# Moving 64 token steps of a router tile to the next stage, in a hybrid decoder kernel with single-neuron experts

## The reference, cut to what matters

```
def peer(x, w_q, keys, u_tab, v_tab):
    ...
        q = einsum('td,de->te', xb, w_q)                     # 8 heads, two halves
        s = einsum('thcd,hcnd->thcn', q, keys)               # 128 scores per half
        sv, si = lax.top_k(s, 16)                            # top 16 of each half
        cv, ci = lax.top_k(all sums of two halves, 16)       # 16 experts per head
        idx = i1 * 128 + i2
        gate = softmax(cv)
        act = gelu(einsum('thkd,td->thk', u_tab[idx], xb))   # dot with a row of u per expert
        return einsum('thkd,thk->td', v_tab[idx], gate * act) # weighted sum of rows of v
```

## Time and profile before

| | us |
|---|---|
| median of 3 runs (5188.72 to 5211.97) | 5198.52 |
| the profiled execution | 5198.58 |
| its span | 5196.8 |
| mean granted TensorE clock | 0.802 |
| busy PE / DVE / POOL | 3423.1 / 3351.0 / 2704.2 |

### The profile page before, as it was taken

One profiled execution on the slowest core, in us unless ns is written; L12 is line 12 of the kernel. 1 busy time (PEld: TensorE's weight loads), 2 busy tenths in 40 slices (PEclk: granted clock), 3 DMA queues, 4 the chain that ended last, 5 costly groups with the idle time before them and its releaser, 6 DMA issues. The chain is left out here.

```text
span 5196.8 us, 52661 instructions
## 1 busy us (share of the span) xinstructions
PE 3423.1 (66%) x17388; PEld 1932.9 (37%) x17388; DVE 3351.0 (64%) x7219; ACT 726.6 (14%) x2591; POOL 2704.2 (52%) x2288
## 2 busy tenths in 40 slices
PE   7887466699785666566499977467566536656206
PEld 6574352354551541442244463163154113211001
DVE  4345896578535985786577543797687657785480
ACT  2131210111310210200122121110111010000000
POOL 1000566466433775774365534466676565426676
PEclk9998678799887778778699988787777765578658
DMA  5543678899766889999799757789998986759768
GB/s 192 170 143 114 216 239 323 295 401 351 286 243 251 318 311 372 352 322 354 273 352 333 287 212 291 292 278 346 377 337 322 356 307 221 279 205 386 262 222 332
DMA packets 467260, 1497.00 MB, mean 288 GB/s; under 512 B 60096, under 2 KB 122240, under 8 KB 454416
## 3 DMA queue, kind: packets, MB, share of 16 engines
q0 software_dynamic: 324864, 1141.04, 59.6%
q1 hardware_dynamic: 120912, 330.01, 17.2%
q10 hardware_dynamic: 21216, 22.60, 1.3%
HBM read 1480.07 MB, written 55.29 MB: 295 GB/s over the span
## 5 line engine op out<-in xcount | busy, mean ns | idle before, releaser
L2027 POOL DMA_INDIRECT e_ring<-peer_u,e_idx x1152 | 1458.7, 1266 | 1090.9 <-issue 526.6
L2027 POOL DMA_INDIRECT e_ring<-peer_v,e_idxT x1104 | 1196.5, 1084 | 1025.2 <-PE e_ff L2179 509.8
L2063 DVE CUSTOM_DVE_ANT_0 e_ring<-e_ring,e_x 128x1024 f32<-128x1024 f32 (+1 forms) x1152 | 1380.4, 1231 | 302.6 <-DMA e_ring<-peer_u,e_idx 294.8
L2179 PE MATMUL e_ff<-e_ring,e_strips 128*32 128x512 f32 x4416 | 726.3, 756 | 611.8 <-DMA e_ring<-peer_v,e_idxT 500.9
L351 PE MATMUL p_ps<-p_hT,p_w 128*128 128x256 f32 (+2 forms) x1728 | 567.6, 483 | 0.0
L2179 PEld LDWEIGHTS e_ff<-e_ring,e_strips 128*32 128x32 f32 x4416 | 163.8, 126 | 1066.9 <-issue 1065.1
L351 PEld LDWEIGHTS p_ps<-p_hT,p_w 128*128 128x128 f32 x1728 | 327.6, 195 | 208.1 <-issue 129.5
L1314 PE MATMUL bank<-wbuf,kqb 128*128 128x512 f32 (+1 forms) x544 | 278.1, 666 | 101.3 <-DMA wbuf<-w_out 101.1
L1400 PE MATMUL bank<-wbuf,kqb 128*128 128x512 f32 (+1 forms) x576 | 275.5, 628 | 21.5 <-DMA wbuf<-wc 21.5
L375 PE MATMUL p_ps<-p_w,p_hT 128*128 128x512 f32 (+1 forms) x576 | 253.5, 603 | 0.0
L1816 DVE MAX8 top<-kb_kdec 128x8 f32<-128x128 f32 (+1 forms) x144 | 40.3, 280 | 330.2 <-ACT kb_kdec L1541 330.2
(11 more groups left out here) (334 smaller groups left out, 4446.1 us busy)
## 6 DMA issues: line engine op xcount, KB each, us to landing
p_w<-w_in SPq DMA_DIRECT2D x156, 512.0 KB, 7.4
wbuf<-w_out SPq DMA_DIRECT2D x72, 1024.0 KB, 9.5
wbuf<-wc SPq DMA_DIRECT2D x72, 1024.0 KB, 8.1
e_ring<-peer_u,e_idx POOLq DMA_INDIRECT x1152, 6.3
e_ring<-peer_v,e_idxT POOLq DMA_INDIRECT x1104, 6.8
rows<-p_tok SPq DMA_DIRECT2D x72, 192.0 KB, 8.2
rows<-rows SPq DMA_DIRECT2D x8, 1280.0 KB, 8.9
z<-p_zs SPq DMA_DIRECT2D x32, 256.0 KB, 6.3
```

The source lines that it names most:

```text
L2027: g.indirect_dma_start(out=self.ring[:, i % RING, :], out_offset=None, in_=table[:, :], in_offset=at, bounds_check=NEXP - 1, oob_is_err=Fa ...
L2063: v.tensor_tensor_reduce(out=self.ring[0:U, i, :], in0=self.ring[0:U, i, :], in1=self.x[0:U, :], scale=1.0, scalar=0.0, op0=ALU.mult, op1= ...
L2179: last = nc.tensor.matmul(self.ff[i][32 * j:32 * j + 32, :], self.strips[:, self.strip_of[t] % NSTRIP, j, 31 - s:63 - s], self.ring[:, sel ...
```

## The change

Tile 3's and tile 6's token steps are cut at token 32 and no longer at token 64. The stages of tiles 4 and 7 do 32 of them in their heads, where they did 64; the third projection and the packed stage do 96 in their tails, where they did 64. The sum of all gathers, of all batches and of all other work is the same.

```
-        mix(4, tail=(2, 80, P), u=3, head=(3, 0, 64))
-        stage([5, 6, 7, LAST], tail=(3, 64, P), u=4)
+        mix(4, tail=(2, 80, P), u=3, head=(3, 0, 32))
+        stage([5, 6, 7, LAST], tail=(3, 32, P), u=4)
         mix(5, head=(4, 0, P))
         mix(6, u=5, head=(5, 0, 80))
-        mix(7, tail=(5, 80, P), u=6, head=(6, 0, 64))
-        mix(LAST, tail=(6, 64, P), u=7, head=(7, 0, P))
+        mix(7, tail=(5, 80, P), u=6, head=(6, 0, 32))
+        mix(LAST, tail=(6, 32, P), u=7, head=(7, 0, P))
```

## The result

The changed kernel takes 5265.63 us (median of 4 runs, 5256.98 to 5266.41) against 5201.94 for the kernel before on the same chip: ratio 1.0126, 95% interval 1.0105 to 1.0146, so +55 to +76 us. The prediction was 5236 us with a range up to 5258: slower, as forecast, but by more. On another chip the same two kernels gave 1.009 (1.007 to 1.011, experiment 7). The profiled execution took 5266.41 us.

The account below looks back on a forecast made before the run. Bounds were read by stage: DVE in the routing end, PE in the third projection, POOL's gathers at the packed stage's empty checkpoints. -12.0 - 8.1 + 21.0 + 36.5 = +37.4 on 5198.6 gave 5236 us, range 5226 to 5256.

Parts of the forecast that it names:

- Part 1: Routing end of tiles 4 and 7: two batches fewer between each one's score blocks, 5.5 and 6.5 us, together -12.0.
- my floor of 4: Routing end of tiles 4 and 7: least gain, 4 us, if the weight loads take most of it.
- My signs of being wrong: Packed-stage gathers under 1.3 us, PE waiting for landed gathers in the projection, or routing end shrinking much beyond its batches.
- Part 2: End of tile 4's and 7's stages: DVE, no longer the last batch, ends the stage; 4.1 us each, -8.1.
- Part 3: Third projection: 8 more batches on PE within the same 30 blocks, 2.56 us each, taken as +21.0.
- Rival C: Third projection already at its DMA limit: 16.8 MB more take 46 us, not 21; total 5261, chance 0.08.
- Part 4: Packed stage: 12 more gathers in each half's bound stretch at POOL's 1.355 us, plus later ones, together +36.5.
- rival A: Packed stage hides its 32 steps in the state products, costing about +5; total 5205, chance 0.08.
- Rival B: Stages last as long as their gathers: tiles 4 and 7 win 44 and 47 us; total 5165, chance 0.03.

Follow-up runs that it names:

- experiment 7: The changed kernel measured again on another chip, against the kernel before: 1.009 (1.007 to 1.011), +48 us.
- 1: The kernel before with only the first pair changed (tile 4's head 32, third projection's tail 96): 1.0037, +19.5 us.
- 2: The kernel before with only the second pair changed (tile 7's head 32, packed stage's tail 96): 1.0069, +36.4 us.
- 8: The changed kernel with four checkpoints inside each half's KS/QS products, given the tail's weight of the empty checkpoints: 1.0047 to the kernel before.
- 9: The kernel before with four checkpoints inside each half's KS/QS products, given the tail's weight of the empty checkpoints: 0.9947.
- experiment 10: The changed kernel with no weight for the packed stage's tail at "prep", so no early batch: 5333.86 us, one run.
- 11: The kernel before with eight checkpoints in each half's KS/QS products and state updates, given the tail's weight of levels 1 to 6: 0.9927.
- 12: The changed kernel with eight checkpoints in each half's KS/QS products and state updates, given the tail's weight of levels 1 to 6: 1.0034 to the kernel before.

## Why the prediction was right and wrong

**Part 1, fewer batches between the score blocks (-12.0): this step failed.** It measured 0.0 and -1.8. Over eight experiments with the whole loads (1, 2 and 7 to 12), first to last top 16 was 42.6 us on average with four batches and 41.8 with two in tile 4, 43.6 and 41.4 in tile 7. I divided the difference between tile 4 and tile 0 by four batches, as if each batch cost the same. But the wait of 1.49 us in the earlier trace rows was tile 0's sign that the loads are just behind the pace without batches, and a batch taken out of such a gap leaves the gap. Even my floor of 4 for the two tiles, made for this case, was high. Without the loads a batch was worth 2.5 us, my figure. The four parts came out 16.7 us above the 37.4 forecast (54.1), and this one step is 10.2 of that. My signs of being wrong had only a routing end that shrinks by more than its batches; it shrank by less.

A wait has a second price: the two blocks after the 4.70 us took 10.07 us in place of 7.13. They are the same 16 matmuls. Windows of the changed kernel over the two blocks before the wait, the two behind it and the next two show what differs, in the third column from the end:

```profile
2411.40:2419.20 7.80, 7.80 (x20) 3.31 (x16) 0.00 (x0) 0.00 (x0) 3.97 (x4) 0.91 0.63 191
2424.00:2434.00 10.00, 10.00 (x16) 3.98 (x16) 2.58 (x13) 0.00 (x0) 0.00 (x0) 0.71 0.43 160
2437.00:2444.00 7.00, 6.85 (x16) 2.67 (x15) 4.20 (x22) 0.11 (x1) 3.96 (x4) 1.00 0.78 265
```

The granted clock fell to a mean of 0.71 behind the wait, so for part of the two blocks PE ran at 1.2 GHz, and they took 2.9 us more. It is no single case: behind the 14 waits of 3.7 to 5.5 us for a load, in tiles 4 and 7 of the traces with 32 head steps there, two blocks took 8.5 to 10.1 us.

**Part 2, the stage's end (-8.1): right in kind.** The time from L1886 to the next stage's first matmul fell from 6.4 and 6.0 us to 2.55 in both tiles, -7.3. In the experiments too it is 2.5 with 32 steps, and 6 to 11 with 64 (9.8 on average in tile 4, 8.3 in tile 7), so that there the part was worth 13 us and not 8.

**Part 3, third projection (+21.0): mechanism right, the sum 3 to 4 low.** It measured +28.0, +28.8 and, with half loads, +21.2; over all traces the stage is 508.2 us with 96 steps (eight traces) and 483.1 with 64 (six), +25.1. A block with a batch takes 9.44 us and one without 2604.10 - 2597.43 = 6.67, so a batch costs 2.77 and not 2.56: I had taken the block alone from a place where 6.77 held a little of the batch. Eight are 22.2. The first block, where the clock is still below full as I had said, takes 8.6 us instead of 6.7. From the first to the last transposes of the 36 blocks (L335) it is 300.2 us against 276.1, +24.1, and the other traces repeat it: 300.0 to 301.1 with 96 steps, 276.1 to 277.0 with 64. The other 4 us of the first pair lie ahead of the first transposes and are mostly scatter. The matmuls of L307 there took 9.50 us in the profile before and 12.61 in the one after, but both lengths come with either tail: about 12.6 in three of the six traces with 64 steps and in four of the eight with 96. On average the first transposes come 0.8 us later with 96. Rival C is out: the windows show 394 and 396 GB/s at a share of 1.02, and no PE wait for a landed gather.

**Part 4, packed stage (+36.5): the sum right to 0.1 us by luck, two of its terms wrong in opposite directions.** First half +21.2, forecast 14.3; second half 302.4 - 145.4 less 272.8 - 124.2 = +8.4, forecast 16.3; from there to `h` +7.0, forecast 5.9. I had it that an earlier batch at "prep" frees the ring and wins back 2.03 us. It does the reverse: the ring's fifth slot, which POOL needs for gather 17, is then held by that batch, which PE does only once its own work up to "prep" is done, and the wait is 7.28 us. Without the batch a row of u lies in that slot. So the first half costs 12 x 1.355 + (7.28 - 2.03) = 21.5, and 21.2 was measured; experiment 10 takes the batch away and gets 4.8 back. In the second half POOL's wait between the halves fell from 19.80 to 13.07 us, so 6.7 of its 16.3 were covered, which leaves 9.6 against the 8.4 measured. I had counted 82 gathers issued by then and 98, which is right, but had not looked at when POOL stood still. Experiments 8 to 12 show the mechanism itself in the first halves, where fewer gathers ahead of the last empty checkpoint make it come earlier at about POOL's pace. They also show how far rival A holds: with checkpoints in them the products have room for some of the steps, not for all.

Rival B is out as well: the stages of tiles 4 and 7 fell by 4.9 and 5.6 us and not by 44 and 47.

**The sum.** With part 1 at -1.8, part 2 at -7.3, part 3 at +25 and part 4 at +36.6 the change costs about 52 us. With the means of the experiments' own traces (-3, -13, +24.5 and +38) it is 47. That fits the +48 of experiment 7 and, less closely, the halves' +56. The first chip's +65 holds about 10 us more that lie in stages the change doesn't touch.

## What to carry to other kernels

A piece of work that stands between two others is not worth its own duration if a transfer is on its way in the same gap. Before it is priced, ask when the transfer behind it was issued and when it lands: here some 8 us after the buffer came free, whatever PE computed meanwhile. And where two engines share a ring, moving a batch to an earlier checkpoint can hold the ring longer, since it is the consumer's arrival there that frees it. Work that only needs a gather belongs beside steps that keep another engine busy: eight more checkpoints in each half of the packed stage, with the tail's steps dealt to them, made the kernel before 0.7% faster.

## What of the hardware I had not expected

A weight load of 1024 KB took 4.6 to 5.0 us from issue to landing where no gathers ran, and 8.1 at the median of all 72; half of it, beside gathers, took 8.04 where the whole had taken 8.06. A PE wait of 4.70 us lengthened the 7.13 us of work behind it to 10.07, the granted clock at 0.71 over that work and 1.00 again over the next two blocks. And the DMA engines of this one core carried 396 GB/s over 160 us, with indirect gathers making up most of it.
